# Who issues a hybrid decoder's K-cache page transfers: ScalarE's hardware queue in place of GpSimd's software queue

## The reference: what is computed

```python
def ada_modulation(c, w_ada, b_ada):
    m = jax.nn.silu(c) @ w_ada + b_ada
...
    h = rms_norm(x, g_pre) * (1.0 + scale) + shift
    z = h @ w_in
    q, k, v, u = jnp.split(z, [ATTN_WIDTH, 2 * ATTN_WIDTH, 3 * ATTN_WIDTH], axis=-1)
...
        k_past = cache_k[l, page_table].reshape(DEC_BATCH, PAST_LEN, N_HEADS, 2, HEAD_DIM)
        v_past = cache_v[l, page_table].reshape(DEC_BATCH, PAST_LEN, N_HEADS, V_DIM)
        k_all = jnp.concatenate([k_past.astype(k.dtype), k], axis=1)
...
        attn = diff_attend(q, k_all, v_all, pos_s, pos_keys_s, lam)
```

## Time and profile before

| | us |
|---|---|
| median of 3 runs | 1496.23 |
| lowest and highest of them | 1493.62, 1498.73 |
| the profiled execution, its whole time | 1494.64 |
| its span, first to last instruction | 1493.0 |
| PE busy in the span | 1446.6 (97%) |
| ACT, DVE, POOL busy | 517.5, 799.7, 102.9 |
| sample stage, turns 0 to 3 | about 312 to 396 of the span |
| median time to landing of a K page, a V page, half a weight chunk | 9.3, 6.9, 5.0 |

### The profile page before, as it was taken

How to read it: one execution, slowest core, us unless ns; L and a number is a source line. 1 busy time by engine, 2 the same in 40 slices (tenths; PEclk the granted TensorE clock), 3 DMA queues, 4 the chain that set the end, 5 groups by cost and what they waited for, 6 DMA issues and landing times.

```text
span 1493.0 us, 26969 instructions
## 1 busy us (share of the span) xinstructions
PE 1446.6 (97%) x10274; PEld 1313.3 (88%) x10274; DVE 799.7 (54%) x1258; ACT 517.5 (35%) x733; POOL 102.9 (7%) x177
## 2 busy tenths in 40 slices
PE   5999999999899998999999999999999999999996
PEld 1777777778588877999998999999999999999996
DVE  2655558856756568665334444333554344445554
ACT  2222233434456445333322333332333232333331
POOL 1000000067410000000000000000000000000002
PEclk9999999999999999999999999999999999999998
DMA  9999988889687777444445544445544444444431
GB/s 366 345 326 323 325 305 318 284 308 360 226 321 257 258 256 248 141 152 158 143 160 200 176 160 148 147 162 185 192 158 144 157 151 141 143 155 152 141 113 71
DMA packets 87880, 316.40 MB, mean 212 GB/s; under 512 B 12176, under 2 KB 12432, under 8 KB 87168
## 3 DMA queue, kind: packets, MB, share of 16 engines
q1 hardware_dynamic: 79200, 287.87, 56.1%
q0 software_dynamic: 5216, 22.51, 4.1%
q10 hardware_dynamic: 3392, 5.01, 0.9%
HBM read 309.56 MB, written 5.80 MB: 211 GB/s over the span
## 4 chain that ended last, share of the span: by engine, by line
PE 83%; DMA 6%; DVE 3%; POOL 2%; issue 2%; ACT 2%; POOLq 1%; SPq 0%; DVEq 0%; ACTq 0%
PE bank L1538 69%; PE bank L1609 7%; DMA raw<-in_stream 4%; PE bank L1500 3%; PE bank L1515 2%; DMA k_pages<-in_kc 1%; DMA pools_out<-u 1%; DMA pool_w<-in_w_pool 1%; ACT w_hi L390 1%; DVE w_lo L782 1%; PE bank L1861 1%; POOLq L1377 0%; POOL win L1396 0%; POOL win L1398 0%; ACT pair L639 0%
## 5 line engine op out<-in xcount | busy, mean ns | idle before, releaser
L390 ACT ACTIVATE w_hi<-raw 128x1024 fp32r<-128x1024 f32 x352 | 361.8, 1054 | 352.8 <-PE bank L1538 232.8
L782 DVE TENSOR_TENSOR w_lo<-raw,w_hi 128x1024 fp32r<-128x1024 f32 x352 | 419.6, 1225 | 117.1 <-ACT w_hi L390 114.9
L1538 PE MATMUL bank<-m_hi,w_hi 128*128 128x320 f32 x1280 | 397.4, 310 | 1.0 <-issue 0.6
L1538 PE MATMUL bank<-m_hi,w_lo 128*128 128x320 f32 x1280 | 395.5, 309 | 0.0
L1538 PE MATMUL bank<-m_lo,w_hi 128*128 128x320 f32 x1280 | 395.5, 309 | 0.0
L1538 PE MATMUL bank<-h_hi,w_hi 128*128 128x320 f32 x1216 | 379.2, 312 | 0.0
L1538 PE MATMUL bank<-h_hi,w_lo 128*128 128x320 f32 x1216 | 375.7, 309 | 0.0
L1538 PE MATMUL bank<-h_lo,w_hi 128*128 128x320 f32 x1216 | 375.7, 309 | 0.0
L1538 PEld LDWEIGHTS bank<-m_hi,w_hi 128*128 128x128 f32 x1280 | 240.3, 188 | 15.0 <-issue 15.0
L1538 PEld LDWEIGHTS bank<-h_hi,w_hi 128*128 128x128 f32 x1216 | 228.2, 188 | 23.2 <-issue 23.2
L1538 PEld LDWEIGHTS bank<-m_lo,w_hi 128*128 128x128 f32 x1280 | 240.3, 188 | 0.0
(11 more groups left out here) (237 smaller groups left out, 1095.3 us busy)
## 6 DMA issues: line engine op xcount, KB each, us to landing
raw<-in_stream SPq DMA_DIRECT2D x544, 512.0 KB, 5.0
k_pages<-in_kc POOLq DMA_DIRECT2D x16, 512.0 KB, 9.3
v_pages<-in_vc POOLq DMA_DIRECT2D x16, 512.0 KB, 6.9
x<-in_x_cm ACTq DMA_DIRECT2D x1, 2560.0 KB, 12.2
x<-in_x_cm POOLq DMA_DIRECT2D x1, 2560.0 KB, 10.8
v_out<-v_cm POOLq DMA_DIRECT2D x1, 1280.0 KB, 9.5
k_out<-back POOLq DMA_DIRECT2D x1, 1280.0 KB, 10.2
y_out<-x SPq DMA_DIRECT2D x2, 640.0 KB, 3.0
```

The source lines that it names most:

```text
L390: act.activation(w_hi[2 * (j % 2) + h][:, :], raw[slot][:, h * 1024:(h + 1) * 1024], ACT.Copy).then_inc(hi_ready, 1)
L782: dve.tensor_tensor(w_lo[q][:, :], raw[slot][:, h * 1024:(h + 1) * 1024], w_hi[q][:, :], ALU.subtract).then_inc(slot_used[slot], 1)
L1538: last = pe.matmul(bank[j % 2][:, 0:T], w[q][:, k * P:(k + 1) * P], v[:, 8 * h + k, :], start=(h == 0 and k == 0 and n == 0), stop=(h == 1 ...
```

## The change

The K pages of pairs 1, 2 and 3 are issued by ACT, in turns 0, 1 and 2, behind the second `hi_fill` of the turn and ahead of `evac_fill`. POOL issues none of them, and goes from `ds_done` straight to picking the queries. The first pair's K pages and all V pages stay on POOL. The transfers of ACT count on two semaphores of their own, `k_again`, one for each sequence of a pair, and PE's scores wait on these from pair 1 on. Nothing else moves.

```diff
+    k_again = [S("k_again0"), S("k_again1")]
...
@@ scalar, behind the exponentials and hi_fill(fills[0] + 1, 1), ada_fill(fills[0])
+            if pr < 3:
+                act.wait_ge(ds_done, pr + 1)
+                act.wait_ge(pg_loaded, 16)
+                for b in (2 * pr + 2, 2 * pr + 3):
+                    for pg in range(PAGES):
+                        n = b * PAGES + pg
+                        page = act.value_load(pages_sb[0:1, n:n + 1], min_val=0, max_val=kc.shape[0] - 1)
+                        act.dma_start(k_pages[:, b % 2, pg, :], kc[ds(page, 1), :, :].rearrange("a p n -> p (a n)")).then_inc(
+                            k_again[b % 2], 16)
             if pr == 1:
...
@@ gpsimd
             pool.wait_ge(ds_done, pr + 1)
             if pr < 3:
-                for b in (2 * pr + 2, 2 * pr + 3):
-                    load_pages(kc, k_pages, b, k_loaded)
                 pick_queries(pr + 1)
@@ tensor, sample_scores
             for par in range(2):
-                pe.wait_ge(k_loaded[par], 32 * (pr + 1))
+                if pr:
+                    pe.wait_ge(k_again[par], 32 * pr)
+                else:
+                    pe.wait_ge(k_loaded[par], 32)
```

## The result

| | us |
|---|---|
| changed kernel, median of 8 runs | 1504.74 (1500.48 to 1510.95) |
| kernel before, median of 8 runs | 1496.74 (1493.62 to 1498.73) |
| ratio, 95% interval | 1.0047 (1.0030 to 1.0064) |
| the profiled execution of the changed kernel | 1510.95, its span 1509.2 |

The change costs 8.0 us. The new median, 1504.74, lies above the predicted range, which ended at 1500.0. The profiled execution is the longest of the eight, so its total is not the place to read the loss from: its span is 16.2 us longer than that of the profile of before. Its first K scores start at 319.11, where those of before started at 312.37, so 6.7 us of the 16.2 lie ahead of anything that the change touches. To compare a position with one of before, I take off these 6.74 us.

The account below looks back on a forecast made before the run. PE, busy for 97% of the span, was taken as the bound. Terms of -1.3 (K wait), +1.0 (V pages) and +0.3 (`pool_w`) summed to 0; the median's 1496.2 less 0.2 gave 1496.0 us, range 1493.0 to 1500.0.

Parts of the forecast that it names:

- What comes late next: Turn 2: store behind K pages delays POOL's tile and pair 3's V pages; PE's V wait 1.0 us, `pool_w` wait +0.3.
- The sum: All terms on PE: POOL, ACT, turns 0 and 1 at 0, turn 2 -1.3, V pages +1.0, `pool_w` +0.3: 0.
- The order of the last wait: End of the stage: `pool_w` lands last, at 397.6, so PE resumes at 397.67 exactly as before.
- the K wait of turn 2: PE's wait for pair 3's K pages: forecast to go, -1.3 us, with the last page landing at about 378.9.
- rival 2: Turn 2: the K wait stays because the DMA engines are full, whoever issues; 1496.2 us, up to 1.5 more; chance 0.22.
- the rule: DMA: all issuing engines' transfers share the same 16 engines, so the change alone is worth nothing, 1496.2 us.
- Rival 3: Turns 0 to 2: K pages land late on ACT's queue, 7.9 us more waits, 1504 us; chance beyond 0.3% 0.09.
- POOL's relief: POOL gains 4.7 us in each of three turns by not issuing K pages; worth nothing by itself.
- ACT's page issue: On ACT: 1.0 us a page, 4.0 us a turn, bounds 1.4 to 6.8 us; price on PE 0.
- turns 0 and 1 without a K wait: Pairs 1 and 2: K pages land in time, 0 taken; bound 1.6 us in turn 0, 2.2 us late possible in turn 1.

Follow-up runs that it names:

- before, late store: Kernel before, all K pages on POOL, only the two stores of fill 13 held back on ACT until fill 14's copy: 1505.22 us, 1.0056.
- stores first: The change, with ACT's block of K pages moved behind `evac_fill`, so the stores stand ahead of it: 1503.97 us, 1.0049.
- clock kept: The change, plus 30 small unused products on PE ahead of its wait for pair 3's V pages: 1502.21 us, 1.0037; again 1500.07 us, 1.0016.
- V pages before the tile: The change, with POOL issuing V pages between the two pooling tiles of turns 1 and 2, not behind both: 1496.72 us, 1.0000.
- pair 3 on POOL: The change for pairs 1 and 2 only; pair 3's K pages stay on POOL as in the kernel before: 1498.08 us, 1.0001.
- no stores: The change without the stores of fills 10, 11 and 13 and without POOL's waits for them: 1496.18 us, 0.9985.

## Why the prediction was wrong

**The step that failed is "What comes late next".** It named the mechanism: store behind K pages, POOL's tile behind the store, V pages behind the tile. It sized it at a V wait of 1.0 us, and the chip showed 7.2. In the positions of before:

| | before | forecast | measured |
|---|---|---|---|
| last K page of pair 3 lands | 381.3 | 378.9 | 381.5 |
| store of fill 13 lands | 377.1 | 380.4 | 384.5 |
| first V page of pair 3 issued | 380.13 | 382.5 | 387.7 |
| a V page's time to landing | 4.4 to 7.5 | up to 7.5 | 9.3 to 10.7 |
| PE's V wait | 0 | 1.0 | 7.2 |
| PE's `pool_w` wait | 1.6 | 1.9 | 0 |

- *K pages, 2.6 us late.* I let them have half of the engines from 370 on, as the V pages of pair 2 would be through. These were not. Their times to landing went to 10.8 us in the median and 14.8 at most (last issued at 368.7 of the profile of after). Two causes are in the traces: POOL had waited 5.7 us for the store of turn 1, so these V pages left up to 2 us later than before, and three queues shared the engines. How much each did is not shown. The last K page took 15.9 us, not the 10 to 11 that I forecast.
- *The store behind them, another 1.5 us.* I took the distance behind `pool_w` in the earlier trace rows, 1.5 us; behind the K pages it was 3.0, and 2.1 to 3.6 in the other five profiles with these pages on ACT ahead of it.
- *POOL from there to the V page, another 1.1 us.* Two operations and an issue took 3.1 us from 391.38 to 394.46, not 2.1.
- *The V pages' own landing, up to 3.2 us more.* I took the longest row of before, 7.5 us. Here they took 9.3 to 10.7 us, in "before, late store" as well, and 6.2 to 14.3 in the second profile of the change. What they meet is shown below the list.
- *The clock.* The sum had no term for it. I counted an idle microsecond of PE as one microsecond; after 7 us of idleness the work behind it ran at the 1.2 GHz level for about 12 us.
- *The order of the last wait.* I had `pool_w` as the last to land, and a delay of V pages as hidden behind it. With V pages that late, `pool_w` was there first: its wait of 1.6 us was swallowed, the only thing that was given back.
- *A slip in the sum.* 1.65 MB behind 370 at the rate that I took is 378.6 and not 378.9. That moves the forecasts behind it by 0.3 us and decides nothing.

**What the late V pages met.** The traces show it: `pool_w`, a load of 1 MB that ACT issues at 394.9, 0.4 us behind the first of them. The DMA view of 394 to 406:

```profile
q1 hardware_dynamic: 491, 1.75, 40.0%
q0 software_dynamic: 476, 1.76, 35.9%
q10 hardware_dynamic: 418, 1.11, 23.5%
```

In "stores first" the V pages left as late, 74.6 us behind the first K scores (75.4 in the change), but `pool_w` only at 86.7, and the weight stream (q1) had 3.3% of the engines from 388 to 397: the pages landed in 4.3 to 4.8 us. I had seen that the two loads would meet, and let only `pool_w` pay for it. `pool_w` took 9.8 us, as before (9.7), and the V pages took longer. No run separates what `pool_w` and what the stream did to them.

**Whether the K wait of turn 2 goes is not settled.** It was forecast as gone. It is 1.6 us in this profile of the change and 1.9 in the second one, but 0 and 0.3 in the two profiles of "clock kept", which is the same program up to that point, and by position the last K page landed at 380.0 to 382.0 in these four, for 381.3 before. It is absent in "V pages before the tile", too. In the first profile rival 2 was nearer: the page quoted with it, "DMA: Bandwidth & Descriptors" of the Trainium skill, section "Issuing engines are not separate DMA queues", has the issuing engines' transfers on the same 16 engines, and the last K page landed at 381.5, for 381.3 before. For the whole change the rule was the wrong guide: who issues a transfer does matter, through what stands behind it on that queue.

**Rival 3 had the sign and the size (1504), but not the cause.** Its K waits were to grow by 7.9 us; they grew by 0.4. "V pages before the tile" removes the loss without touching the K pages. The variant "stores first" shows that rival 3's mechanism exists, at 7.9 us of K waits in all, when the pages leave still later.

**Right** were: POOL's relief, worth nothing; ACT's page issue, 1.0 us forecast, where the profile has 276 to 480 ns for the value load and 349 ns for the transfer, so that the transfers of a turn start 1.0 to 1.3 us apart (turn 1: 343.6 to 347.1), and its cost to PE, none ("V pages before the tile" has it all and is level); turns 0 and 1 without a K wait. The last K page left at 372.3 - 6.7 = 365.6 rather than at 368.7, as ACT issued the first page ahead of its copy `w_hi` and the second before that copy had ended; it landed late all the same.

**Is there a gain in the change at all?** None that was found. With the harm taken out it measures 1.0000 (V pages before the tile) and 1.0001 (pair 3 on POOL); "no stores" at 0.9985 leaves work out. No kernel tried is measurably faster than the one before.

## What to carry to other kernels

Moving a large transfer to another queue puts it ahead of whatever that queue carried, and a small store can be the thing that matters: ask who waits for the store's landing, and what that engine issues next. Here 2 MB ahead of a 60 KB store cost 8 us through a third engine, and issuing the needed pages ahead of the waiting tile took the cost away. Price a new wait of the matrix engine with the clock that it may lose. Take landing times from a stretch in which as many queues are busy, and when two loads are moved into each other's way, price the delay for both.

## What the runs showed of the hardware

- Three queues with work shared the 16 DMA engines in about thirds (36.8, 32.9 and 32.1% in one microsecond). A store of 128 x 120 floats issued behind four pages took 14.0 to 17.4 us to land in six profiles, for 10.0 in the kernel before.
- V pages of 512 KB took 9.3 to 10.7 us to land beside `pool_w` and the weight stream (queue shares 35.9, 23.5 and 40.0%), and 4.3 to 4.8 us where neither stood in their way (stores first).
- ACT's sequencer issued page transfers while ACT was still busy. In turn 0 the first started at 326.45, inside the copy from 326.07 to 327.12. In turn 2 it started at 369.17, ahead of the copy that stands before it in the program (369.37 to 370.42).
- After PE had stood still from 399.1, the granted clock was 0.94 in 400 to 404, 0.50 from 404 to 416, and 0.86 in 416 to 420.
